# Row totals of rotated features in a latent expansion: exact float32 passes against float32r passes over split squares

## What is computed

```python
q = (_rmsnorm_2(c_q, q_a_norm_w) @ w_uq).reshape(b, s, 4, 192)
q_nope, q_rope = q[..., :128], q[..., 128:]
q_rope = q_rope * cos[:, None, :] + _rotate_half(q_rope) * sin[:, None, :]
kv = (_rmsnorm_2(c_kv, kv_a_norm_w) @ w_ukv).reshape(b, s, 4, 256)
k_nope, v_mla = kv[..., :128], kv[..., 128:]
k_rope = k_rope * cos + _rotate_half(k_rope) * sin          # one for all four heads
q_m = _rmsnorm_2(jnp.concatenate([q_nope, q_rope], axis=-1), mla_q_norm_w)
k_m = _rmsnorm_2(jnp.concatenate([k_nope, k_rope], axis=-1), mla_k_norm_w)
```

## Time and profile before

| | |
|---|---|
| three runs | 3077.36 us median (3076.13 to 3078.94) |
| the profiled execution, its own time | 3070.93 us |
| its span, first to last instruction | 3069.1 us |
| PE busy | 2956.1 us, 96% |
| DVE busy | 2025.9 us, 66% |
| POOL busy | 1607.5 us, 52% |
| ACT busy | 1239.1 us, 40% |
| mean granted TensorE clock | 0.991 of full speed |
| the chain that ended last, PE's share | 67% |

### The profile page before, as it was taken

How to read it: one execution, slowest core, us unless ns; L and a number is a source line. 1 busy time by engine, 2 the same in 40 slices (tenths; PEclk the granted TensorE clock), 3 DMA queues, 4 the chain that set the end, 5 groups by cost and what they waited for, 6 DMA issues and landing times.

```text
span 3069.1 us, 39500 instructions
## 1 busy us (share of the span) xinstructions
PE 2956.1 (96%) x12984; PEld 2316.3 (75%) x12984; DVE 2025.9 (66%) x2970; ACT 1239.1 (40%) x1988; POOL 1607.5 (52%) x1019
## 2 busy tenths in 40 slices
PE   8999998999999999999899999999999899999997
PEld 7788785668877778888788677578667688877886
DVE  7899965645344777777548632456984766675658
ACT  4321215620335544444222332455774466652221
POOL 3254433324442378888679334472002477777877
PEclk9999999999999999999999999999999999999999
DMA  3122410025120244444984122634422277789774
GB/s 124 38 89 96 148 59 14 1 97 200 53 69 21 96 162 164 164 164 168 346 300 158 51 90 103 195 97 104 100 66 89 92 268 260 260 313 346 264 255 174
DMA packets 156607, 449.30 MB, mean 146 GB/s; under 512 B 17084, under 2 KB 28516, under 8 KB 155720
## 3 DMA queue, kind: packets, MB, share of 16 engines
q1 hardware_dynamic: 128656, 369.68, 35.2%
q10 hardware_dynamic: 27832, 78.08, 6.9%
HBM read 298.25 MB, written 148.13 MB: 145 GB/s over the span
## 4 chain that ended last, share of the span: by engine, by line
PE 67%; issue 10%; POOL 9%; DVE 8%; ACT 3%; DMA 1%; SPq 0%; POOLq 0%; ACTq 0%; DVEq 0%
PE ps L1162 18%; PE ps L1164 18%; PE ps L1163 18%; POOL left_lo L855 5%; POOL part_in L850 3%; PE ps L1212 2%; PE ps L1405 2%; PE ps L1824 1%; PE ps L1812 1%; DVE sums_t L3298 1%; PE ps L1395 1%; PE ps L1797 1%; PE ps L1798 1%; DVE tmp L2883 1%; DMA part_in<-mlp_weights_dram 1%
## 5 line engine op out<-in xcount | busy, mean ns | idle before, releaser
L855 POOL TENSOR_TENSOR left_lo<-part_in,left_hi 128x512 fp32r<-128x512 f32 x414 | 575.2, 1403 | 251.5 <-ACT left_hi L2686 92.0
L744 POOL TENSOR_TENSOR w_hi<-w_raw,zero 128x1024 fp32r<-128x1024 f32 x70 | 134.9, 1928 | 496.0 <-PE ps L1164 491.4
L850 POOL TENSOR_TENSOR part_in<-part_in,part_in 128x512 f32<-128x512 f32 x252 | 359.8, 1428 | 38.4 <-DMA part_in<-mlp_weights_dram 17.8
L747 POOL TENSOR_TENSOR w_lo<-w_raw,w_hi 128x1024 fp32r<-128x1024 f32 x70 | 194.6, 2780 | 5.5
L1162 PE MATMUL ps<-h_hi,w_hi 128*128 128x512 f32 x480 | 188.5, 393 | 5.9 <-DVE h_lo L2877 5.9
L1163 PE MATMUL ps<-h_lo,w_hi 128*128 128x512 f32 x480 | 187.4, 390 | 0.0
L1164 PE MATMUL ps<-h_hi,w_lo 128*128 128x512 f32 x480 | 187.4, 390 | 0.0
L1162 PE MATMUL ps<-down_t,left_hi 128*128 128x512 f32 x432 | 170.5, 395 | 8.6 <-DVE part_t L3203 4.1
L774 POOL TENSOR_TENSOR w_hi<-w_raw,zero 128x512 fp32r<-128x512 f32 x5 | 7.7, 1540 | 322.1 <-PE ps L1164 322.1
L1163 PE MATMUL ps<-down_t,left_hi 128*128 128x512 f32 x432 | 169.2, 392 | 0.0
L1164 PE MATMUL ps<-down_t,left_lo 128*128 128x512 f32 x432 | 169.1, 391 | 0.0
(11 more groups left out here) (605 smaller groups left out, 8667.9 us busy)
## 6 DMA issues: line engine op xcount, KB each, us to landing
w_raw<-weights_dram SPq DMA_DIRECT2D x102, 512.0 KB, 3.3
part_in<-ffn_weights_dram SPq DMA_DIRECT2D x144, 256.0 KB, 3.2
part_in<-mlp_weights_dram SPq DMA_DIRECT2D x144, 256.0 KB, 4.5
mlp_parts_scratch<-part_t SPq DMA_DIRECT2D x64, 512.0 KB, 4.7
down_t<-mlp_parts_scratch SPq DMA_DIRECT2D x64, 512.0 KB, 6.8
ffn_parts_scratch<-part_t SPq DMA_DIRECT2D x44, 512.0 KB, 4.6
down_t<-ffn_parts_scratch SPq DMA_DIRECT2D x44, 512.0 KB, 6.1
mlp_parts_scratch<-part_b SPq DMA_DIRECT2D x32, 512.0 KB, 5.1
```

The costliest lines, as they stand in the source:

```text
L744: nc.gpsimd.tensor_tensor(w_hi[s][:], raw[s][:], zero[:, 0:1].broadcast_to([P, 1024]), ALU.add).then_inc(w_rounded, 1)
L747: nc.gpsimd.tensor_tensor(w_lo[s][:], raw[s][:], w_hi[s][:].bitcast(F32), ALU.subtract).then_inc(w_split, 1)
L850: tt(part_in[p][dst][:], part_in[p][dst][:], part_in[p][other][:], ALU.add).then_inc(left_summed, 1)
L855: tt(lo[:], src[:], hi[:].bitcast(F32), ALU.subtract).then_inc(w_split, 1)
```

## The change

The rope squares are no longer summed as float32. They are split in a high and a low part, both float32r, and `over_features` runs on these:

- For the keys, the two copies of the rope rows serve as two parts: `k_rope_parts` holds the high part in partitions 0 to 63 (ACT copies all 128) and the low part in partitions 64 to 127 (DVE overwrites them). One pass with a float32r matrix of ones sums both.
- For the queries, `q_rope_hi` (ACT copy) and `q_rope_lo` (DVE subtraction) are two tiles, and each total takes two passes, with `halves_r`.
- `halves_r` and `ones_r` are float32r copies of the constants, made by DVE.
- `q_rope_hi` lies at BR + 36 KB, the place of `head_raw0` and `head_raw1`. SP gets a wait, ahead of the first load of head 1: `g_tot` of all eight steps.
- The other pass of each total, over `tmp`, stays float32.

```diff
+        halves_r = at("halves_r", AR + 61 * KB + 512, [P, 3, P], F32R)
+        ones_r = at("ones_r", AR + 63 * KB, [P, P], F32R)
+        k_rope_parts = at("k_rope_parts", AR + 24 * KB, [P, S], F32R)
+        q_rope_hi = at("q_rope_hi", BR + 36 * KB, [P, 2, S], F32R)
+        q_rope_lo = at("q_rope_lo", AR + 48 * KB, [P, 2, S], F32R)
...
                     if hd == 1 and i == 0:
                         sp.wait_ge(head_split, 5)
+                        sp.wait_ge(g_tot, 2 * MLA_HEADS)
...
             def head_total(e):
 
-                if e == 0:
-                    pe.wait_ge(rope_sq, 3)
-                elif e >= 2:
+                if e in (0, 1, 5):
+                    pe.wait_ge(rope_lo, 1 + (0, 1, 5).index(e))
+                if e >= 2:
                     pe.wait_ge(g_rs, e - 1)
                 hd, is_q = e // 2, e % 2
-                rope = q_rope_sq[:, hd // 2, :] if is_q else k_rope_sq[:]
-                over_features(wide(2 + e % 2), rope, halves[:, 1 + (hd % 2 if is_q else 0), :], True, False)
+                if is_q:
+                    over_features(wide(2 + e % 2), q_rope_hi[:, hd // 2, :], halves_r[:, 1 + hd % 2, :], True, False)
+                    over_features(wide(2 + e % 2), q_rope_lo[:, hd // 2, :], halves_r[:, 1 + hd % 2, :], False, False)
+                else:
+                    over_features(wide(2 + e % 2), k_rope_parts, ones_r[:], True, False)
...
             act.wait_ge(c_free, 4)
-            nc.scalar.activation(k_rope_sq[:], k_rope[:], ACT.Square).then_inc(rope_sq, 1)
+            step(nc.scalar.activation(k_rope_sq[:], k_rope[:], ACT.Square))
...
             store_rest(2 * DIFF_HEADS - 1)
+            act.wait_ge(d_stored[0], 32 * DIFF_HEADS)
+            nc.scalar.activation(k_rope_parts[:], k_rope_sq[:], ACT.Copy).then_inc(rope_hi, 1)
...
             for p in range(2):
                 act.wait_ge(r_free, p + 1)
-                nc.scalar.activation(q_rope_sq[:, p, :], q_rope[:, p, :], ACT.Square).then_inc(rope_sq, 1)
+                step(nc.scalar.activation(q_rope_sq[:, p, :], q_rope[:, p, :], ACT.Square))
+                if p == 0:
+                    nc.scalar.activation(q_rope_hi[:, p, :], q_rope_sq[:, p, :], ACT.Copy).then_inc(rope_hi, 1)
...
             head_square(0)
+            nc.scalar.activation(q_rope_hi[:, 1, :], q_rope_sq[:, 1, :], ACT.Copy).then_inc(rope_hi, 1)
...
             dve.wait_ge(tables_in, 48)
+            nc.vector.tensor_copy(halves_r[:], halves[:])
+            nc.vector.tensor_copy(ones_r[:], ones[:])
...
+            lanes = slice(ROPE, P)
+            dve.wait_ge(rope_hi, rope_hi_0 + 1)
+            tt(k_rope_parts[lanes, :], k_rope_sq[lanes, :], k_rope_parts[lanes, :].bitcast(F32), ALU.subtract).then_inc(rope_lo, 1)
+
             dve.wait_ge(w_used, SLABS["diff_value"][0] + 4)
...
                 nc.vector.tensor_copy(v_value[:, j, :], ps[:, j, :]).then_inc(v_dve, 1)
+            for p in range(2):
+                dve.wait_ge(rope_hi, rope_hi_0 + 2 + p)
+                tt(q_rope_lo[:, p, :], q_rope_sq[:, p, :], q_rope_hi[:, p, :].bitcast(F32), ALU.subtract).then_inc(rope_lo, 1)
```

More of the change, by code:

```diff
@@ L505, in program @@
         right_scaled, scaled_0 = m_probs, 2 * MEM_HEADS
+        rope_hi, rope_hi_0, rope_lo = in_hi, 4, rope_sq
         right_formed, right_hi, right_lo, right_0 = n_tmp, n_hi, n_lo, sum(n for n, _ in PRE.values())
```

## The result

The changed kernel takes 3081.45 us (median of 20 runs, 3077.43 to 3088.71), the kernel before 3076.53 us (20 runs, 3072.68 to 3086.64). The ratio is 1.0018 [1.0012, 1.0024]: 5.5 us slower, between 3.7 and 7.4. So it is slower, clear of noise, yet the middle of the interval stays within the 0.2% named ahead. The profiled execution took 3078.75 us, its span 3077.0 us: 7.9 us more than the span before.

A forecast was written before the change was run, and what follows sets the result against it. PE, busy 96% of the span, was taken as the bound, level with square, Exp, `g_nope` in the steps. -0.4 + 0.1 + 6.0 + 2.4 = +8.1 us gave 3085.5 us, range 3078.5 to 3089.5.

The forecast's parts named there:

- The steps inside: nothing: Expansion steps before the last total: 8.2 us less PE work shortens them by nothing, as `g_nope` still releases expand.
- Rival B: Expansion steps: the rope passes are on the path, steps shrink by 8.2 us, sum +0.3 us; chance 0.08.
- two level paths: Between expands: PE's own two passes take as long as square, Exp, `g_nope`, which has no rope pass in it.
- The last total, -0.4 us: End of the expansion: the last total has no step behind it and comes 0.4 us sooner.
- The start, +0.1 us: Ahead of the first head square: ACT's added copy and wait slip the start by 0.1 us; other added work is covered.
- SP's wait, +6.0 us: Head 1's seven loads wait for the last total, splits end late, and PE waits 6.0 us at logits(8).
- The clock, +2.4 us: After PE's wait at logits(8): a lowered granted clock costs 2.4 us (1.7 to 2.5).
- Rival C: After PE's wait: the clock stays up, sum +5.7 us, 3083.1; chance 0.12.
- A: Head 1's loads land in time: PE waits 0.9 us, sum +0.6 us, 3078.0; chance 0.20.
- D: Rope passes: float32r calls are no cheaper, query steps get 1.7 us longer each; chance 0.02.
- The sum: Whole kernel: the terms give +8.1 us, profiled execution 3070.93 to 3079.0 us, median 3077.36 to 3085.5 us.

The follow-up runs named there:

- b2: The kernel before without the rope pass in each of the eight totals: 3072.79 us against 3077.22, ratio 0.9988.
- b3: The kernel before with ACT's Exp moved directly behind its Ln: 3073.23 us against 3077.22, ratio 0.9983.
- b1: The kernel before with only SP's wait for all eight totals added ahead of head 1's first load: 3083.27 us against 3075.81, ratio 1.0024.
- a3: The changed kernel with 24 small unused float32 matmuls on PE ahead of its wait for head 1's splits: 3079.65 us against the kernel before's 3075.81, ratio 1.0012.
- a1: The changed kernel with the query high parts laid elsewhere, so SP needs no wait: 3074.38 us against the kernel before's 3075.81, ratio 0.9994.
- a2: The changed kernel with head 1's rope pieces and values loaded first, only the plain tiles behind the wait: 3073.68 us against the kernel before's 3075.81, ratio 0.9992.
- a4: a1 with ACT's Exp moved directly behind its Ln: 3067.80 us, ratio 0.9970 to the kernel before.
- c1: The changed kernel run again with no edit: 3082.73 us against the kernel before's 3077.22, ratio 1.0018.
- a5: a2 with ACT's Exp moved directly behind its Ln: 3069.33 us, ratio 0.9976 to the kernel before.
- d1: The changed kernel, SP's wait kept, with ACT's Exp moved directly behind its Ln: 3077.79 us against the kernel before's 3076.21, ratio 1.0005.

## Why the prediction came out as it did

The sign and the place were right: slower, through SP's wait. The size was not quite: 8.1 us forecast, 5.5 timed on the ratio, and 4.9 between the medians. 8.1 is above the interval's end of 7.4. The median of 3081.45 us lies in the stated range, but below the forecast's own (3083 to 3089.5), and slower by over 0.2%, which had 0.60, became 0.18%, just inside what had 0.35. The forecast of 3085.5 is 4.0 us too high; 0.8 of these are the base, 3077.36 us from three runs against 3076.53 from twenty. Step by step:

**The steps inside: nothing.** Right. The stage changed by +0.04 us, expands are still released by `g_nope`, and b2 shows it with all of the rope work gone. Rival B (steps 8.2 us shorter) is excluded in the trace. The reason given, two level paths, was read at step 3 and holds for the early steps; at step 6 the stores' wait for `g_rope` covered the rope pass by 1.38 us already before (see b3), which the prediction did not see.

**The last total, -0.4 us: failed.** It came 50.44 us after the first `v_value` copy (1940.32 to 1990.76) instead of 50.51, 0.07 us sooner. The pass over `tmp` in step 7 does start 0.4 us sooner after its expand, as forecast, and waits 0.21 us for its square. But the expand of step 7 itself starts 46.31 us after the first copy instead of 45.94. Of these 0.37 us the slip of the start is 0.12, as seen at the expand of step 5 (32.55 against 32.43); the rest arises in steps 5 and 6, where PE waits 0.82 and 2.34 us for squares that stand behind ACT's stores, and these wait for `g_rope` (2.46 us long at step 3, 2.56 at step 4).

**The start, +0.1 us.** About right: DVE's first `g_nope` comes 13.94 us after the first `v_value` copy, 13.79 before. The work said to be covered was covered. Its sum was miscounted: the text lists five instructions of DVE, not four, so 5 x 1.23 + 2 x 1.05 = 8.3 us; the two casts took 0.36 and 0.22 us.

**SP's wait, +6.0 us.** The stall is 6.20 us. The gate was put at 1992.0 and is 1992.84; landing at 13.6 us behind it and is 13.9. The sum of parts was partly luck. The prediction let the rope pieces move at 224 GB/s and 1.2 MB of stores compete. The four stretches after 1994 hold 3.0 x (292 + 315 + 404 + 373) = 4.15 MB: nearly all of the 2.6 MB of loads and of the 1.57 MB of stores, at 346 GB/s. So more bytes moved than assumed, and faster than 224 GB/s. The two misses cancelled.

The 224 GB/s was also read wrongly. The stretch from 1987 to 1990 is not one with little but rope pieces in it: the values left at 1987.38 and two stores right behind, the first of which is

```profile
1987.39 0.35 ACTq L2557 DMA_DIRECT2D mla_nope_scratch<-g_nope  x1
```

The stretch before it moved 268 GB/s; SP issued the four rope pieces from 1983.81 to 1987.33:

```profile
1984.00:1987.00 3.00, 2.72 (x9) 1.33 (x8) 2.47 (x2) 1.62 (x2) 2.22 (x1) 1.00 1.00 268
```

So neither row is a rate of rope pieces alone, and the comparison of 224 with a page's 196 GB/s settles nothing.

 The Trainium skill, "DMA: Bandwidth & Descriptors", section "Anatomy of one DMA", has 2.0 us plus bytes at 436 GB/s for one DMA (measured on GpSimd's path). Taken for all the loads as one, an estimate, that is 8.0 us; measured were 13.9. Taken for the 4.2 MB that moved it would give 11.6 us, so by this estimate the stores are 3.6 of the 5.9 us between. The page "SBUF — State Buffer", section "Door 1: The DMA port swizzle", puts 64-partition transfers at 196 GB/s. No run here has such transfers alone. In the trace the first two stretches, with rope pieces in flight among stores and other loads, moved 292 and 315 GB/s, the third 404; at 404 the bytes of the two would have taken 4.5 us instead of 6.0. So a lower rate there cost at most some 1.5 us, and whether the rope pieces made it is not shown.

**The clock, +2.4 us.** 2.7 in the changed kernel's trace, 1.4 in b1's, and nothing in a3, where PE was kept busy. Rival C is excluded in the profiled executions, and so are A (the splits end at 2028.5, not before 2023) and D (0.46 us a call).

**The sum: the weakest step.** In the trace the stall and the clock come to +8.9 us and the span grew by 7.9, with 1.7 us less behind `diagonal` in it, so the terms were sized well for the profiled execution. What did not hold is to carry them over to the median one to one. The timed runs divide the loss so: the change without its wait is -1.4 us [-4.6, +0.9], and the wait on top of that 0.24% between two ratios, 7.4 us; in b1, the wait alone, 7.5 us [4.6, 10.5]. By these the wait is sized right (8.4 forecast with its clock), and the surplus is in the rest, forecast at -0.3 us. But a1's interval holds -0.3 too, and no trace shows a place where 1.4 us are gained. b2 hints the same way, 3.7 us gained in timed runs with none in the stage. Where such a gain lies wasn't found; that stays open. The twenty timed executions of the kernel before differ by up to 14 us, and its profiled one (3070.93 us) was shorter than all of them.

## What to carry to other kernels

When a tile moves into the place of another, count all that stands behind the new wait in the same list, and let only the loads that touch the place stand there: the order of the loads was worth the whole stall (a2). Before PE's work in a software pipeline is made cheaper, look at who releases its next step; where PE and another path are level, less work on one gives nothing (b2), and first the other has to be shortened, here by moving one Exp (b3), after which both help (a4). And read more than one step: here the late ones were held by another engine than the early ones.

## What the hardware did that I had not expected

Less work for PE brought a low clock in the late steps. In a1, PE alone (as the earlier trace rows):

```profile
1984.40:1988.40 4.00, 1.65 (x4) 0.83 1.01 388
1988.40:1992.00 3.60, 3.60 (x10) 0.71 0.89 245
```

PE was busy for 1.65 of 4.0 us, and then worked at a granted clock of 0.71, partly at the 1.2 GHz level. ACT's Ln of step 6 waits 2.80 us for the total there, against 1.13 in the changed kernel's first profile, and that accounts for the 1.0 us by which a1's stage is longer. b2 and c1 have such a stretch as well (c1's stage is 58.32 us), a2 too. Of the kernels with less work for PE and the old order of ACT, the first profile of the changed kernel and a3 have none; nor have the kernel before, b1, b3, a4, a5 and d1. So with the old order of ACT the saved work can turn into idle time that costs more than its length, in some executions and not in others. That may also be a part of why timed differences and the stage don't agree, but this wasn't shown.
